# A shorter VectorE row in the turned LayerNorms, expert choice ahead of the exponential, and idle TensorE products in four waits

## The reference

```python
for l in range(DEPTH):                                  # 2 layers
    y, ... = token_mixer(h, ...)                        # projections, sparse attention, DeltaNet, merge
    h = layer_norm(DEEPNORM_ALPHA * h + y, ln1_g[l], ln1_b[l])
    f = swiglu(h, ...) if l % 2 == 0 else moe_ffn(h, router, w1, w3, w2)
    h = layer_norm(DEEPNORM_ALPHA * h + f, ln2_g[l], ln2_b[l])

def moe_ffn(h, router, w1, w3, w2):
    logits = h @ router                                 # 8 experts
    top_val, top_idx = lax.top_k(logits, 2)
    top_w = jax.nn.softmax(top_val, axis=-1)
    gate = sum(one_hot(top_idx, 8) * top_w[..., None])
    return sum(gate[..., e] * swiglu(h, w1[e], w3[e], w2[e]) for e in range(8))
```

## Time and profile before

| | us |
|---|---|
| three runs | 2036.63, 2034.21, 2035.61 |
| median | 2035.61 |
| profiled execution, its own time | 2036.27 |
| span of the profile | 2034.3 |
| TensorE busy | 1950.3 |
| VectorE busy | 1355.8 |
| ScalarE busy | 1062.5 |
| GpSimd busy | 85.1 |

### The profile page before, as it was taken

How to read it: one execution, slowest core, us unless ns; L and a number is a source line. 1 busy time by engine, 2 the same in 40 slices (tenths; PEclk the granted TensorE clock), 3 DMA queues, 4 the chain that set the end, 5 groups by cost and what they waited for, 6 DMA issues and landing times. The chain is left out here.

```text
span 2034.3 us, 25919 instructions
## 1 busy us (share of the span) xinstructions
PE 1950.3 (96%) x10571; PEld 1641.5 (81%) x10571; DVE 1355.8 (67%) x1550; ACT 1062.5 (52%) x1206; POOL 85.1 (4%) x149
## 2 busy tenths in 40 slices
PE   6999999899989999998999999999999999999995
PEld 5677879899976778887888888888888888888884
DVE  3744146644334643265597988979889798797986
ACT  2233233444322324244576776767767677676773
POOL 4002000200020011001000000000000000000000
PEclk9999999899989999999799999999999999999998
DMA  7223225355422232153399999999999999999992
GB/s 205 83 87 93 63 75 185 125 166 166 151 72 87 80 112 81 50 157 124 124 372 330 345 365 307 374 335 343 368 303 376 335 339 371 304 374 338 338 373 106
DMA packets 260479, 456.89 MB, mean 225 GB/s; under 512 B 32218, under 2 KB 111274, under 8 KB 260356
## 3 DMA queue, kind: packets, MB, share of 16 engines
q1 hardware_dynamic: 258966, 454.74, 65.2%
q10 hardware_dynamic: 1390, 0.44, 0.1%
HBM read 452.11 MB, written 3.04 MB: 224 GB/s over the span
## 5 line engine op out<-in xcount | busy, mean ns | idle before, releaser
L380 DVE TENSOR_TENSOR wl<-ring,wh 128x2048 fp32r<-128x2048 f32 x385 | 880.6, 2289 | 256.9 <-ACT wh L374 253.6
L374 ACT ACTIVATE wh<-ring 128x2048 fp32r<-128x2048 f32 x385 | 737.2, 1917 | 322.0 <-PE ps L349 322.0
L349 PE MATMUL ps<-hT,ring 128*128 128x288 f32 (+1 forms) x1376 | 360.7, 414 | 10.9 <-ACT hT L660 8.2
L349 PE MATMUL ps<-wh,xgh 128*128 128x512 f32 x896 | 355.3, 397 | 2.4 <-DVE wl L380 2.4
L349 PE MATMUL ps<-wh,xgl 128*128 128x512 f32 x896 | 350.1, 391 | 0.0
L349 PE MATMUL ps<-wl,xgh 128*128 128x512 f32 x896 | 349.7, 390 | 0.0
L349 PEld LDWEIGHTS ps<-hT,ring 128*128 128x128 f32 (+1 forms) x1376 | 253.7, 190 | 85.4 <-issue 15.5
L349 PEld LDWEIGHTS ps<-wh,xgh 128*128 128x128 f32 x896 | 168.7, 188 | 40.2 <-DVE wl L380 5.7
L349 PEld LDWEIGHTS ps<-wh,xgl 128*128 128x128 f32 x896 | 168.5, 188 | 36.2
L349 PEld LDWEIGHTS ps<-wl,xgh 128*128 128x128 f32 x896 | 168.9, 188 | 33.6
L349 PE MATMUL ps<-wh,gEh 128*128 128x512 f32 x448 | 143.5, 401 | 0.0
(11 more groups left out here) (405 smaller groups left out, 2412.7 us busy)
## 6 DMA issues: line engine op xcount, KB each, us to landing
ring<-in_moe_w SPq DMA_DIRECT2D x336, 1024.0 KB, 5.3
ring<-in_w_in SPq DMA_DIRECT2D x38, 1024.0 KB, 5.2
ring<-in_ffn_w SPq DMA_DIRECT2D x33, 1024.0 KB, 5.2
ring<-in_w_out SPq DMA_DIRECT2D x8, 1024.0 KB, 5.2
ring<-in_w_in SPq DMA_DIRECT2D x32, 128.0 KB, 3.1
ring<-in_w_oa SPq DMA_DIRECT2D x16, 256.0 KB, 3.9
ring<-in_w_ob SPq DMA_DIRECT2D x8, 512.0 KB, 4.9
resid<-in_x_prompt SPq DMA_DIRECT2D x1, 1024.0 KB, 5.2
```

Source lines behind the costliest of these rows:

```text
L349: ins = nc.tensor.matmul(*a, **k)
L374: nc.scalar.activation(wh[:, k % WS, :], ring[:, s:s + SLOT], ACT.Copy).then_inc(hi_ready, 1)
L380: ins = nc.vector.tensor_tensor(wl[:, k % WS, :], ring[:, s:s + SLOT], wh[:, k % WS, :].bitcast(F32), ALU.subtract)
```

## The change

- In the turned norms GpSimd subtracts the mean from tiles 0 to 4 (`XC_POOL = 5`, was 4 to 7), and VectorE from tiles 5 to 7, each just ahead of that tile's product and linked to it. VectorE's row up to the reciprocal holds the variance alone.
- `idle_products(times)`: float32 products of the identity with the identity repeated to 512 columns, into bank 7, which nobody reads. Five at the head of TensorE's queue in `dense_mlp`, in `front(1)` and in `moe`, and two between the position products and the wait of the first gather. (`norm` and `front(0)` call it with 0.)
- The choice of experts no longer waits for the Exp; the weights and gates are computed after `low_half(1)`.
- The split of the low halves in `dense_mlp` keeps its four and four (`HL_DVE = 4`).

```diff
-        XC_DVE = 4
+        XC_POOL = 5
+        def idle_products(times):
+            for _ in range(times):
+                nc.tensor.matmul(ps[7][:], ident[:], ident[:].unsqueeze(1).to_broadcast([P, 4, P]), start=True, stop=True)
 ...
         def centred(pool, q):
             pool.wait_ge(nst_ready, 2 * q + 2)
-            for k in range(XC_DVE, KD):
+            for k in range(XC_POOL):
                 nc.gpsimd.tensor_tensor(hT[:, k, :], hT[:, k, :], mean, ALU.subtract).then_inc(xc_ready, 1)
 ...
         def normalised(dve, c, q):
-            dve.wait_ge(nst_ready, 2 * q + 2)
-            for k in range(XC_DVE):
-                c(nc.vector.tensor_tensor(hT[:, k, :], hT[:, k, :], mean, ALU.subtract))
             dve.wait_ge(nstd_ready, q + 1)
             c.link(nc.vector.reciprocal(rsd, sdev))
             for k in range(KD):
-                if k >= XC_DVE:
-                    dve.wait_ge(xc_ready, (KD - XC_DVE) * q + k - XC_DVE + 1)
+                if k < XC_POOL:
+                    dve.wait_ge(xc_ready, XC_POOL * q + k + 1)
+                else:
+                    c.link(nc.vector.tensor_tensor(hT[:, k, :], hT[:, k, :], mean, ALU.subtract))
                 nc.vector.tensor_tensor(tn[:, k, :], hT[:, k, :], rsd, ALU.mult).then_inc(tn_ready, 1)
 ...
+                    idle_products(5 if l else 0)      # front(l), TensorE
                     sw = slot(u0, (8, 80))
 ...
+                    idle_products(5)                  # dense_mlp, TensorE
                     have_split(pe, n0 + 1)
 ...
+                    idle_products(5)                  # moe, TensorE
                     pe.wait_ge(lgt_in, 16)
 ...
                     ins.then_inc(pos_done, 1)
+                    idle_products(2)
                     pe.wait_ge(pos_ready, 1)
 ...
-                    dve.wait_ge(rt_exp, 1)            # moe, VectorE
-                    c.link(V.tensor_scalar(rw[:, :, 2:3], rw[:, :, 1:2], 1.0, None, ALU.add))
-                    c.link(V.reciprocal(rw[:, :, 2:3], rw[:, :, 2:3]))
-                    c.link(V.tensor_tensor(rw[:, :, 3:4], rw[:, :, 2:3], rw[:, :, 1:2], ALU.mult))
 ...
-                    c(V.tensor_tensor(gate, rsel[:, :, 0:NE], each(rw[:, :, 2:3]), ALU.mult))
-                    c(V.tensor_tensor(gate2, rsel[:, :, NE:2 * NE], each(rw[:, :, 3:4]), ALU.mult))
                     ins = V.tensor_tensor(selm, rsel[:, :, 0:NE], rsel[:, :, NE:2 * NE], ALU.add)
                     ins.then_inc(sel_ready, 1)
-                    c.sync()
-                    c(V.tensor_tensor(gate, gate, gate2, ALU.add))
 ...
                     onehot(0)
                     low_half(1)
+                    dve.wait_ge(rt_exp, 1)
+                    c.link(V.tensor_scalar(rw[:, :, 2:3], rw[:, :, 1:2], 1.0, None, ALU.add))
+                    c.link(V.reciprocal(rw[:, :, 2:3], rw[:, :, 2:3]))
+                    c.link(V.tensor_tensor(rw[:, :, 3:4], rw[:, :, 2:3], rw[:, :, 1:2], ALU.mult))
+                    c(V.tensor_tensor(gate, rsel[:, :, 0:NE], each(rw[:, :, 2:3]), ALU.mult))
+                    c.link(V.tensor_tensor(gate2, rsel[:, :, NE:2 * NE], each(rw[:, :, 3:4]), ALU.mult))
+                    c.link(V.tensor_tensor(gate, gate, gate2, ALU.add))
```

More of the change, by code:

```diff
@@ L607, in _ @@
                 def _(pe):
+                    idle_products(0 if final else 0)
                     for k in range(0 if final else KD):
@@ L2052, in program @@
                                                        sem("gT_ready"))
+        HL_DVE = 4
         hf_ready, hl_dve, hl_pool = sem("hf_ready"), sem("hl_dve"), sem("hl_pool")
@@ L2065, in _ @@
                     centred(pool, 0)
-                    for k in range(XC_DVE, KD):
+                    for k in range(HL_DVE, KD):
                         pool.wait_ge(h_ready, k + 1)
@@ L2086, in _ @@
                                 if u == 0 and c == 0:
-                                    if k < XC_DVE:
+                                    if k < HL_DVE:
                                         pe.wait_ge(hl_dve, k + 1)
                                     else:
-                                        pe.wait_ge(hl_pool, k - XC_DVE + 1)
+                                        pe.wait_ge(hl_pool, k - HL_DVE + 1)
                                 ins = rel.mm(ps[2 * u + c][:, 0:T], w0[u][0][:, k, P * c:P * c + P], hTl[:, k, :],
@@ L2165, in _ @@
                                                 ALU.mult, ALU.add).then_inc(hf_ready, 1)
-                    for k in range(XC_DVE):
+                    for k in range(HL_DVE):
                         dve.wait_ge(h_ready, k + 1)
@@ L2434, in _ @@
                     centred(pool, 2)
-                    pool.wait_ge(xc_ready, 3 * (KD - XC_DVE))
+                    pool.wait_ge(xc_ready, 3 * XC_POOL)
                     for j, h in enumerate((htokh, htokl)):
```

## The result

The changed kernel takes 2013.67 us (median of four runs, 2012.98 to 2016.33) against 2036.12 before: ratio 0.9894, 95% interval 0.9877 to 0.9911. The forecast was 2026.2, with a range down to 2017.5. The profiled execution took 2013.88 us around a span of 2012.2.

The account below looks back on a forecast made before the run. TensorE was taken as the bound, busy 96% of the span, plus its idle and lower-clock stretches. Terms 0 + 3.4 + 6.2 - 0.2 = 9.4 us gave 2026.2 us, with an 8-in-10 range of 2017.5 to 2031.0.

Parts of the forecast that it names:

- the dense MLP (0): Dense MLP behind the first turned norm: no net gain, 0 us (bounds -1 to 2), with GpSimd's low halves held up.
- the gather (-0.2): First gather behind two idle products: lower clock kept, sometimes with a delay, -0.2 us (bounds -1.4 and +6.5).
- rivals (5.4 and 6.7 us, together 2014): GpSimd free in dense MLP, 2020.8, chance 0.13; gather at full clock, 2019.5, chance 0.23; both, chance 0.05.
- GpSimd's hold-up: Dense MLP: GpSimd's third low half stood 4.56 us until VectorE's weight split ended; expected again only 0.6 us earlier.
- The 2.7 us for the lower clock: Behind each norm's wait: TensorE resuming at the lower clock was said to cost about 2.7 us more.
- the 5.4 us of the rival: Dense MLP: gain if GpSimd is not held up in the low halves, 5.4 us, giving 2020.8; chance 0.13.
- Second projection, 3.4: Second norm to first evacuation: earlier tiles with TensorE at full clock gain 3.4 us; 1.2 if the clock is low.
- Router, 3.9: Expert stage: three tiles done before the clock falls, the other five at the lower clock; gain 3.9 us (3 to 5.5).
- Choice, 2.3: Router's end to first gather: choosing experts without waiting for the Exp, 2.3 us; 6.2 us together with the router.
- position products at 3.4 us: Routing: if transposes don't count as clock activity, the skill page's rule, position products cost 3.4 us, gain 0.8 less.
- Idle products, 4.3 us for a group of five: Head of each norm's wait: five float32 products of 512 columns at full clock, 0.87 us each, 4.3 in all.
- too dear: Idle products in the norms' waits cost too much each, making the kernel slower, 2056 at 3.5 us each; chance 0.02.

## Why the prediction was wrong

**The wrong steps are two terms of the sum, the dense MLP (0) and the gather (-0.2), each sized by its pessimistic reading; a third part of the gain was beyond the sum.** Both stood as rivals (5.4 and 6.7 us, together 2014), with a chance of 0.05 for both at once. The sum was 9.4 us, the profiled execution gained 22.1. That 2014 lies 0.3 us from the measured 2013.67 is partly luck: the dense MLP gave 1.2 us less than its rival's price, and falls of the clock elsewhere gave 1.5 that no case had.

- *Dense MLP, forecast 0, measured 4.23.* The step that failed: that GpSimd's hold-up of the earlier trace rows would come again 0.6 us sooner, leave TensorE waiting for 3.8 us and drop its clock. It came in none of the eight profiles with a new norm and GpSimd in the low halves, and in each of the three with VectorE's row as it was before (4.56 us in the kernel before, 5.21 with the idle products alone, 4.54 with the choice alone). One row of one execution was taken as a fixed price. What makes the hold-up is not settled. It goes with pauses in VectorE's row (the run with the waits put into it), but does not return when the row is unbroken (the run with eight subtractions). Nor is it the small offset between the two engines: the held-up low half began 0.10 to 0.13 us ahead of VectorE's instruction, and three of the four in the changed kernel 0.11 to 0.13 ahead, without a hold-up. Its cost with TensorE early was therefore never measured; late, it was 0.
- *Within that term* the split was wrong too. The 2.7 us for the lower clock were counted as if TensorE were alone; without the idle products 0.8 to 1.1 us are lost. The shorter row of the norm, with 3.2 us alone, is the larger share. And the 5.4 us of the rival left out that GpSimd and VectorE slow each other in the low halves: with all eight on VectorE the stretch gained 5.5 us, with four and four 4.2.
- *Gather, forecast -0.2, measured 4.9 and 1.4 to 1.5 behind it.* The step that failed: that the clock would fall among the position products, as in the earlier trace rows, and that two idle products would come too late to save it. The clock was full in them (from 962.39 on), and without the pair it fell only in the wait behind them. The pair prevents that fall: with it the gather took 5.38 or 5.39 us in all nine profiles of the changed kernel and its variants that have the pair, without it 10.27. The 1.4 to 1.5 are half of the 2.9 to 3.0 us that the first expert's products ran at the lower clock in the run without the pair and before; the last stretch as a whole differs by up to 1.8 us between profiles with the same gather, so its 1.65 proves nothing by itself.
- *Second projection, 3.4, measured 3.57.* The sum was right, but the split wasn't: the prediction left 1.2 us if the clock was low. With the clock low for the first 3.8 us of TensorE's work the norm's row alone gained 3.3, and with it low for 5.5 us 2.45. The idle products are worth 0.3 to 1.1.
- *Router, 3.9, measured 4.58.* Right: the clock fell 3.2 us behind the idle products, inside 2.4 to 4.1, and the rest ran at the lower one. In the second profile of the changed kernel it fell 2.3 us behind them, and the gain was 4.0. Without the five 3.0 of it remain.
- *Choice, 2.3, measured 1.67 here and 2.3 alone.* The transposes took 5.2 us, wholly at the lower clock, not 4.4. In the second profile of the changed kernel the clock came back within them (at 960.82), and the gain was 2.4; router and choice together gained 6.25 and 6.39 us in the two profiles, against 6.2 in the forecast. The selection came 2.2 us behind the router's end, as the forecast's times have it (969.2 against 967.0; its words say 1.6). One working there doesn't come out: position products at 3.4 us instead of the 2.2 in the sum would cost 1.2 us, not 0.8. They took 2.0.
- *Idle products, 4.3 us for a group of five, measured 4.53.* A pair at the lower clock took 3.78 us, not 3.5, and was late by 0.6 in the run with the old norm, not by 1.4; in the changed kernel's profile it was at the full clock (1.98) and not late. The rival "too dear" fell.
- *Not in the sum:* 2.55 us between first evacuation and third norm. Before, the clock was low there from 636.74 to 640.15 and from 892.74 to 896.15; no line of that stage changed. The falls come and go: none in the changed kernel's two profiles, one in the norm alone, two stretches and one in the two profiles with eight low halves. I count them as the spread of executions, like the -1.05 ahead of the first norm (a fall at 51.03); together they are 1.5 of the 22.1 us. That the change has no part in them is not shown: the profiles without the idle products in front of the second projection have such a fall in four of five cases, those with them in four of eleven.

## What to carry to other kernels

Here the idle products were worth something only when what they left of the wait was short: a group of five won at most 0.5 us in a wait of 8.2 us, and 0.8 to 1.6 us in one of 5. So shorten the wait first, then cover it. Look also at short waits that stand ahead of work whose time depends on the clock: the two products between the position products and the gather bought 6 us, more than the other fifteen together. And a stall that one trace shows once is a range, not a price.

## What the runs showed of the hardware

- The clock can fall while TensorE is busy: in the router's 8-column products it fell at 952.15, 2.8 us into them, and stayed low to their end.
- It came back in or right behind the 24 transposes: low at 956.99 when they start, full at 962.39 behind them, and in the kernel before full at 974.66, within those that began at 970.87. The gather ran 10.27 us at the lower clock without its coming back, and 5.38 us at the full one without its falling.
- The Trainium skill's page "SBUF — State Buffer" (Who interferes with whom) says that of VectorE and GpSimd the one that issues first gets the shared ports for its whole instruction, and the other waits. Where they took turns it fits: 0.87 us (GpSimd) and 0.91 us (VectorE) beside each other in the changed kernel, against 0.81 and 0.42 alone. The hold-ups of 4.56 and 5.21 us, over five and seven instructions of VectorE, do not fit, since GpSimd's instruction had begun first.
- A reciprocal beside GpSimd's subtractions took 1.95 us, alone 1.94, and a subtraction beside it 0.79 to 0.80 us: neither slowed the other.
